# Four staggered start addresses for the split weight slots of a two-layer hybrid trunk, and operands that start 64 bytes past a multiple of 128

## The reference

```python
for l in range(DEPTH):                       # 2
    u = _rms_norm(x, pre_mix_norm_w[l])
    proj = u @ w_in[l]                       # 1024 x 6864
    ...                                      # conv, SiLU, gated delta rule -> o_a; low-rank attention -> o_b
    y_a = o_a @ w_branch_a[l]                # 1024 x 1024
    y_b = o_b @ w_branch_b[l]                # 1024 x 1024
    h = gates[:, :, 0] * y_a + gates[:, :, 1] * y_b
    x = x + _rms_norm(h @ w_out[l], post_mix_norm_w[l])
    u = _rms_norm(x, pre_ffn_norm_w[l])
    f = jnp.square(jax.nn.relu(u @ w_ff1[l])) @ w_ff2[l]     # 1024 x 4096, 4096 x 1024
    x = x + _rms_norm(f, post_ffn_norm_w[l])
```

## Time and profile before

| | before |
|---|---|
| median of 3 executions | 1116.6 us (1115.73 to 1117.03) |
| the profiled execution | 1117.01 us, of which 1115.2 us lie between its first and its last instruction (the span) |
| TensorE busy: matmuls, weight loads | 94%, 92% of the span |
| VectorE, ScalarE, GpSimd busy | 67%, 50%, 12% |
| mean granted clock of TensorE | 0.974 of full speed |
| read from HBM | 161.25 MB, 146 GB/s over the span |

### The profile page before, as it was taken

How to read it: one execution, slowest core, us unless ns; L and a number is a source line. 1 busy time by engine, 2 the same in 40 slices (tenths; PEclk the granted TensorE clock), 3 DMA queues, 4 the chain that set the end, 5 groups by cost and what they waited for, 6 DMA issues and landing times.

```text
span 1115.2 us, 24120 instructions
## 1 busy us (share of the span) xinstructions
PE 1051.4 (94%) x10552; PEld 1024.9 (92%) x10552; DVE 741.6 (67%) x998; ACT 556.7 (50%) x778; POOL 137.6 (12%) x109
## 2 busy tenths in 40 slices
PE   6899899999998999999898998999999989999996
PEld 5799899899998999999887998998999989999996
DVE  6776568599566787644486756685985767875443
ACT  5575375644544544433354753757355445444431
POOL 6101000220000322100000100003100013221001
PEclk9989999999999999999978999999999999999998
DMA  7344334334565366556434333343345544665561
GB/s 261 109 133 133 98 104 126 114 114 139 182 182 179 99 205 189 187 180 183 133 113 145 120 115 98 115 120 109 124 159 163 179 151 137 204 187 187 184 180 38
DMA packets 45608, 163.85 MB, mean 147 GB/s; under 512 B 5184, under 2 KB 5440, under 8 KB 45504
## 3 DMA queue, kind: packets, MB, share of 16 engines
q1 hardware_dynamic: 44928, 161.50, 46.2%
q10 hardware_dynamic: 576, 0.82, 0.2%
HBM read 161.25 MB, written 1.05 MB: 146 GB/s over the span
## 4 chain that ended last, share of the span: by engine, by line
PE 83%; DVE 7%; ACT 6%; issue 3%; DMA 0%; POOL 0%; POOLq 0%; SPq 0%; ACTq 0%; DVEq 0%
PE dense L552 24%; PE dense L554 23%; PE dense L553 23%; DVE wlo L1293 2%; ACT whi L965 1%; PE sides L911 1%; PE sides L937 1%; PE sides L912 1%; PE sides L793 1%; PE sides L785 1%; DVE utmp L1329 1%; PE sides L947 1%; PE sides L749 1%; PE sides L889 1%; DVE yT L1616 1%
## 5 line engine op out<-in xcount | busy, mean ns | idle before, releaser
L1293 DVE TENSOR_TENSOR wlo<-raw,whi 128x1024 fp32r<-128x1024 f32 (+1 forms) x304 | 399.4, 1323 | 213.9 <-ACT whi L965 213.7
L965 ACT ACTIVATE whi<-raw 128x1024 fp32r<-128x1024 f32 (+1 forms) x304 | 314.9, 1046 | 239.1 <-PE dense L554 231.9
L552 PE MATMUL dense<-uh,whi 128*128 128x256 f32 x768 | 229.7, 299 | 0.0
L554 PE MATMUL dense<-uh,wlo 128*128 128x256 f32 x768 | 221.9, 289 | 2.4 <-issue 2.4
L553 PE MATMUL dense<-ul,whi 128*128 128x256 f32 x768 | 221.9, 289 | 0.0
L552 PE MATMUL dense<-fuh,whi 128*128 128x256 f32 x512 | 146.4, 286 | 9.7 <-DVE ful L1630 9.6
L554 PEld LDWEIGHTS dense<-uh,wlo 128*128 128x128 f32 x768 | 150.6, 196 | 2.8 <-issue 2.8
L552 PEld LDWEIGHTS dense<-uh,whi 128*128 128x128 f32 x768 | 150.7, 196 | 2.6 <-issue 0.8
L553 PEld LDWEIGHTS dense<-ul,whi 128*128 128x128 f32 x768 | 150.8, 196 | 0.3
L554 PE MATMUL dense<-fuh,wlo 128*128 128x256 f32 x512 | 146.0, 285 | 0.0
L553 PE MATMUL dense<-ful,whi 128*128 128x256 f32 x512 | 145.7, 285 | 0.0
(11 more groups left out here) (286 smaller groups left out, 1944.0 us busy)
## 6 DMA issues: line engine op xcount, KB each, us to landing
raw<-weights SPq DMA_DIRECT2D x304, 512.0 KB, 3.7
xT<-x_t SPq DMA_DIRECT2D x4, 256.0 KB, 5.5
out_t<-xT SPq DMA_DIRECT2D x4, 256.0 KB, 2.3
cst<-consts ACTq DMA_DIRECT2D x1, 512.0 KB, 6.5
prm_all<-params ACTq DMA_DIRECT2D x1, 150.0 KB, 4.0
pos_i<-pos ACTq DMA_DIRECT2D x1, 128.0 KB, 5.3
cst<-consts ACTq DMA_DIRECT2D x1, 6.0 KB, 5.6
```

The costliest lines, as they stand in the source:

```text
L552: mm(o_, h_[:, ws], ahi[:, k0 + k, :], start=is_first, stop=False, skip_group_check=True)
L554: x_ = mm(o_, l_[:, ws], ahi[:, k0 + k, :], start=False, stop=is_last, skip_group_check=True)
L965: return A(o_, i_, ACT.Copy)
L1293: TT(wlo[s][:, 0:w], raw[s][:, 0:w], f32(whi[s][:, 0:w]), ALU.subtract).then_inc(lo_ready, 1)
```

## The change

Each of the four slots gets its own remainder by 128: slot i of `whi` and slot i of `wlo` start 32*i bytes past a multiple of 128 (0, 32, 64, 96), and the region behind the kept tiles starts 64 bytes past one. `keep_at` skips the bytes needed for that. No instruction is added, removed or moved; operand addresses alone differ.

```diff
         xT = keep("xT", [P, KD, S])
         raw = [keep(f"raw{i}", [P, PIECE]) for i in range(RING)]
-        whi = [keep(f"whi{i}", [P, PIECE], F32R) for i in range(RING)]
-        wlo = [keep(f"wlo{i}", [P, PIECE], F32R) for i in range(RING)]
+        def keep_at(name, remainder):
+
+            base[0] += (remainder - base[0]) % 128
+            return keep(name, [P, PIECE], F32R)
+
+        whi = [keep_at(f"whi{i}", 32 * i) for i in range(RING)]
+        wlo = [keep_at(f"wlo{i}", 32 * i) for i in range(RING)]
         cst = keep("cst", [P, NCST])
...
-        R0 = base[0]
+        R0 = (base[0] + 127) // 128 * 128 + 64
         KIB = 1024
```

## The result

The changed kernel takes 1110.54 us (median of 20 runs, 1106.5 to 1113.94), the kernel before 1115.51 us in the same comparison (20 runs, 1109.45 to 1119.92). The ratio is 0.995, with a 95% interval of 0.9938 to 0.9963: faster by half a per cent. The forecast was no change. The time lies inside the range of the forecast, on the side of rival C.

A forecast was written before the change was run, and what follows sets the result against it. The pace of TensorE's load and matmul pairs in lines 552 to 554 was taken to bound the kernel. All five parts were taken as 0, so the median stays at 1116.6 us, range 1106 to 1128 us.

The forecast's parts named there:

- rival C: Lines 552 to 554, faster: different remainders keep weight and moving streams apart in memory; 1069 us, partial 1106; chance 0.20.
- What bounds the kernel: TensorE's pace in lines 552 to 554, 7032 matmuls each behind its own weight load, sets the time.
- Part 2: Moving operands, all 64 bytes past: taken as 0; upper end 5.9 us, lower end a gain of 9 ns per step.
- Part 1: Weight loads from `whi` and `wlo`, slots 1 to 3 shifted: taken as 0, upper end 4.4 us.
- Parts 3 and 4: Splits on ScalarE and VectorE: 0, upper end 3.3 us; DMA of `cst` and `prm_all`: 0, at 5% more 0.3 us.
- Rival B: Lines 552 to 554, slower: one extra access, 0.83 ns per shifted operand; 1122.5 us, with weights 1126.9; chance 0.22.
- Rival D: Matmul stretches: addresses only settle which of two known paces applies; 1124.0 us at most or 1114.5; chance 0.08.

The follow-up runs named there:

- h1: Against the kernel before, no stagger: in all slots high halves 128 past a multiple of 256, low halves 0, region 64; 1088.54 us, ratio 0.9744.

## Why the prediction was wrong

*What bounds the kernel*: right. The difference between the two kernels is in the step of lines 552 to 554, and so is nearly all of every difference of the experiments (35 us of it in h1, less 7 elsewhere).

*Part 2, the moving operands*, is the step that failed. It put the term at nothing, with the reason: "I take 0, because the trace has two paces at one set of addresses and the pace doesn't follow the block index". The step then moved by 1.2 ns on average with the change, and by 5.3 ns (119.1 to 113.8) in h1. Both observations in that reason are true. What I made of them is not. The pace didn't follow the block index because blocks step by 512 and 1024 bytes, and all of those leave the distance by 256 as it is. The trace of before held one distance only, and could not speak about others. And two paces at one set of addresses say that a rhythm can be kept from the start of a stretch; they don't say that the addresses have no part in which rhythms there are. The runs have 120.0 at distance 0, 120.0 and 118.65 at 128, 117.8 and 113.3 at 192, 117.8 at 64, and 113.3 alone at 192 with 64. That the time stayed inside the range is in part luck: in the changed kernel one slot gains much, two gain little and one loses.

*Part 1, the weight loads*: line 686 was the wrong neighbour. Its loads stand 4h bytes off and repeat one element, and I read from it that a load off a multiple of 128 costs nothing. For a load by itself that may be so, no run shows it; it is the distance to the moving operand that counts, and line 686 comes four matmuls at a time, too few to settle (slot 0 of the changed kernel needed nine). Nor was 277 against 282 ns nothing: the durations follow the pace, as the medians (the middle number) of the kernel with both at 64 and of h1 show, at 120.0 and 113.3 ns a step:

```profile
L558 PE MATMUL dense<-fh,whi x512: 282/283/284, 463.9 to 1108.9; 128*128 128x256 f32 x171
L558 PE MATMUL dense<-fh,whi x512: 276/276/276, 451.4 to 1074.7; 128*128 128x256 f32 x171
```

So 5 ns of duration is as much as this case's paces differ, and it was read as "no penalty" alone.

*Parts 3 and 4, the splits and the DMA*: right. 1047 and 1324 ns; `cst` lands after 6.4 us and `prm_all` after 4.1, against 6.5 and 4.0.

*Rival C* had the mechanism in the right place, with a fifth of the chance. Its price was off by slot: I wrote that slots 0, 1 and 3 gain and slot 2 doesn't, which takes the distance by 128. Slot 0 gained 4.6 ns, slots 1 and 2 about 1, and slot 3 lost 1.7, in sum 1.2 ns instead of 6.75 (three quarters of 9). Its floor, 110 ns from the earlier trace rows, was near: 113.3 is what the best distances reach. The objection that other engines' streams don't disturb TensorE's stands (the paces hold while VectorE's share changes), but it says nothing of TensorE's own two streams, as the prediction noted itself. *Rival B* (one more access per shifted operand) is not what happened, since both at 64 costs a quarter of a per cent (some 3 us) and not the 11.7 us of one more access on either side in all 7032 steps (0.83 ns twice), and the region or the weights at 64 alone bring a gain; only slot 3 went its way, and its loss has no explanation here beyond its distances. *Rival D* is half right: the paces exist and there are more of them, and a change of address sets which ones. By the two paces of before alone, 119.08 to 118.65 ns in some 6640 steps, at most 3 us could be won; the prediction had 2.1, since it gave the slow pace to the feed-forward block of layer 0 alone, and other stretches had it too.

The Trainium skill, "SBUF — State Buffer", section "Who interferes with whom", has TensorE's two read ports independent and TensorE waiting on nobody. The runs don't agree as far as the pace goes: with nothing but the two operands' distance changed, a step takes 113.3 or 120.0 ns. The 262 cycles (109.2 ns) that the Trainium skill, "TensorE: Matmul & The Clock Gate", section on the back-to-back issue gap, has for 256 columns were reached by no fp32r stretch here; the page gives them for a matmul by itself and says that a stream of load and matmul pairs has another spacing.

What stays open: why the distance works, and why the order of the two halves matters (192 with 64 leaves 113.3 alone, 64 with 192 doesn't). That the loads and the moving reads meet in a part of the memory that repeats every 256 bytes is argued from the distances alone; no run separates the two streams. Distances other than multiples of 32 were not tried.

## What to carry to other kernels

Where a kernel is bound by pairs of a weight load and a matmul on full-size float32r operands, count matmuls per stretch in the profile: a pace some per cent over the columns' time is worth an experiment with the byte distance between the two operands, and it costs one line. Give all slots of a ring the same distance, and try the halves of a split apart: in the changed kernel the stagger over the slots mixed one good distance with three that gave little or cost something. A trace in which every operand has the same remainder says nothing about remainders, however regular it is.

## What the runs showed of the hardware

The step of a load and a matmul of 256 float32r columns at the full granted clock depends on the start of the moving operand minus the start of the weights, by 256: 120.0 ns at 0; 118.65 or 120.0 at 128; 117.8 or 113.3 at 192; 117.8 at 64 in nearly all stretches; in the feed-forward blocks 118.7 at 160 and 118.3 at 224 (one execution); 113.3 alone, once settled, at 192 for the high and 64 for the low halves, 118.9 or 113.3 the other way round, and 118.2 at 192 and 128. Where two are given, a stretch keeps the one into which it settled as long as TensorE doesn't pause and the distance stays, for 170 us in one case. At half the granted clock nothing of it is seen: a step takes 213.4 ns on average in the kernel before, in h1 and in the changed kernel alike. In h1 the starts there are

```profile
11.92 0.41 PE L559 MATMUL dense<-xl,whi 128*128 128x256 f32 x1
12.14 0.41 PE L560 MATMUL dense<-xh,wlo 128*128 128x256 f32 x1
12.35 0.41 PE L558 MATMUL dense<-xh,whi 128*128 128x256 f32 x1
```

0.43 us for two steps, as before.
